# Context projections between the steps of stick attention, an earlier memory attention and a reordered first gated tile

## What is computed

```python
def first_block(...):
    for i in range(2):
        h = rmsnorm(x, mix_norm[i])
        y_mem = memory_cross_attention(q_mem, mem_k, mem_v)
        if i == 0:
            y_main = b_gate * causal_short_conv(c_gate * u, conv_w[i])
        else:
            y_main = stick_breaking_attention(q_sb, k_sh, v_sh)
        x = x + concatenate([y_main, y_mem]) @ w_o[i]
        x = x + swiglu(rmsnorm(x, ffn_norm[i]), w_gate[i], w_up[i], w_down[i])
    return rmsnorm(x, final_norm)

def stick_breaking_attention(q, k, v):          # 12 heads of 64, 128 queries at a time
    z = q @ k.T * scale
    log_not = where(causal, log_sigmoid(-z), 0.0)
    tail = cumsum(log_not, reverse=True) - log_not
    a = where(causal, exp(log_sigmoid(z) + tail), 0.0)
    return a @ v
```

## Time and profile before

| what | value |
|---|---|
| runs | 1219.28, 1216.86, 1215.56 us; median 1216.86 us |
| the profiled execution | 1218.38 us |
| its span | 1217.1 us |
| mean granted clock of TensorE | 0.979 |
| PE busy | 1162.5 us, 96% |
| DVE busy | 833.4 us, 68% |
| ACT busy | 623.2 us, 51% |
| POOL busy | 149.4 us, 12% |
| PE's share of the chain that ended last | 81% |
| DMA engines, share held by the raw loads' queue | 55.6% |
| read from HBM | 219.42 MB, 181 GB/s over the span |

### The profile page before, as it was taken

The page is one execution under the profiler, slowest core; times in us unless marked ns, Lnnn a source line. Parts: engine busy times, 40 slices in busy tenths (PEclk is TensorE's granted clock), DMA queues, the critical chain, the costliest instruction groups (busy, mean ns, idle before and its releaser), DMA issues.

```text
span 1217.1 us, 21837 instructions
## 1 busy us (share of the span) xinstructions
PE 1162.5 (96%) x9014; PEld 1113.4 (91%) x9014; DVE 833.4 (68%) x1278; ACT 623.2 (51%) x938; POOL 149.4 (12%) x111
## 2 busy tenths in 40 slices
PE   8999899999899898999999999999999988999996
PEld 6999899999788788999998898979899988999995
DVE  5677577778774766777778656476645767677775
ACT  5645444445564645444345664655436545555453
POOL 0003000000100012000000000000001032344431
PEclk9999999999998898999999999999999998999998
DMA  8545588777644144777887445354325553555540
GB/s 317 191 158 174 182 268 258 236 251 227 242 132 130 52 163 157 234 247 256 267 270 243 156 156 173 105 160 139 118 88 161 185 177 102 188 177 190 177 153 36
DMA packets 60467, 221.90 MB, mean 182 GB/s; under 512 B 6752, under 2 KB 7008, under 8 KB 59984
## 3 DMA queue, kind: packets, MB, share of 16 engines
q1 hardware_dynamic: 59904, 219.06, 55.6%
q10 hardware_dynamic: 288, 1.05, 0.2%
q0 software_dynamic: 176, 0.39, 0.1%
HBM read 219.42 MB, written 1.05 MB: 181 GB/s over the span
## 4 chain that ended last, share of the span: by engine, by line
PE 81%; DVE 10%; ACT 5%; issue 3%; DMA 1%; SPq 0%; POOL 0%; ACTq 0%; DVEq 0%
PE PS L350 23%; PE PS L352 22%; PE PS L351 22%; PE PS L355 14%; DVE w_lo L1309 3%; ACT w_hi L837 2%; DVE PS L1877 1%; DVE SQ L1575 1%; DMA ARENA<-memT 1%; DVE raw L1331 0%; DVE SQ L1345 0%; DVE ARENA L1345 0%; PE PS L455 0%; DVE H_lo L1355 0%; PE PS L594 0%
## 5 line engine op out<-in xcount | busy, mean ns | idle before, releaser
L1309 DVE TENSOR_TENSOR w_lo<-raw,w_hi 128x1024 fp32r<-128x1024 f32 x325 | 398.9, 1228 | 268.8 <-ACT w_hi L837 268.3
L837 ACT ACTIVATE w_hi<-raw 128x1024 fp32r<-128x1024 f32 x356 | 373.0, 1054 | 144.2 <-PE PS L352 118.4
L350 PE MATMUL PS<-Y_hi,w_hi 128*128 128x256 f32 x1240 | 359.3, 290 | 11.4 <-issue 3.7
L351 PE MATMUL PS<-Y_lo,w_hi 128*128 128x256 f32 x1240 | 354.5, 286 | 0.0
L352 PE MATMUL PS<-Y_hi,w_lo 128*128 128x256 f32 x1240 | 354.3, 286 | 0.0
L350 PEld LDWEIGHTS PS<-Y_hi,w_hi 128*128 128x128 f32 x1240 | 241.7, 195 | 18.0 <-issue 11.8
L351 PEld LDWEIGHTS PS<-Y_lo,w_hi 128*128 128x128 f32 x1240 | 242.1, 195 | 0.4 <-issue 0.2
L352 PEld LDWEIGHTS PS<-Y_hi,w_lo 128*128 128x128 f32 x1240 | 241.7, 195 | 0.0
L350 PE MATMUL PS<-H_hi,w_hi 128*128 128x256 f32 x808 | 232.1, 287 | 7.7 <-DVE G_lo L1436 4.6
L351 PE MATMUL PS<-H_lo,w_hi 128*128 128x256 f32 x808 | 229.1, 284 | 0.0
L352 PE MATMUL PS<-H_hi,w_lo 128*128 128x256 f32 x808 | 229.0, 283 | 0.0
(11 more groups left out here) (207 smaller groups left out, 1323.2 us busy)
## 6 DMA issues: line engine op xcount, KB each, us to landing
raw<-stream SPq DMA_DIRECT2D x404, 512.0 KB, 4.2
ARENA<-memT SPq DMA_DIRECT2D x2, 512.0 KB, 7.6
X<-xT SPq DMA_DIRECT2D x1, 1024.0 KB, 11.2
ARENA<-c_rows SPq DMA_DIRECT2D x2, 512.0 KB, 8.1
ARENA<-memT SPq DMA_DIRECT2D x1, 1024.0 KB, 8.5
ARENA<-ctxT SPq DMA_DIRECT2D x1, 1024.0 KB, 7.3
outT<-ARENA SPq DMA_DIRECT2D x2, 512.0 KB, 2.6
CROW<-c_rows SPq DMA_DIRECT2D x1, 512.0 KB, 10.5
```

The lines of the kernel that those rows point to most:

```text
L350: pe.matmul(o, wh, xh, start=start, stop=False, skip_group_check=True)
L351: pe.matmul(o, wh, xl, start=False, stop=False, skip_group_check=True)
L837: act.activation(w_hi[n % RING][:], raw[at][:], ACT.Copy).then_inc(*mark("hi", n))
L1309: dve.tensor_tensor(w_lo[n % RING][:], raw[raw_of("slot", n)][:], w_hi[n % RING][:], ALU.subtract).then_inc(*mark("lo_dve", n))
```

## The change

It does five things.

- The stages `ctx_lr` and `ctx_k` (5 slots) move from behind `ffn1` to between `kv_v1` and `w_o1`. There they are slots 122 to 126, and steps of stick attention run beside them. Stick outputs become a side task of their own (`stick_outputs`) in PSUM banks 2 and 3. The context set has its own tiles `CX_hi`, `CX_lo`; its sum of squares runs beside `a_c`, its norm in the tail of `ffn0`.
- Memory attention of layer 1 starts with `b_q` at once, where a step of `nothing` and the norm of `kv` stood ahead of it. On ACT and DVE it is run together with that norm by a new helper `both`. The stick schedule follows it, together with the stick outputs.
- In the first tile of each feed-forward, ACT and DVE do the gated product (`hidden`, `g_hi`, `g_lo`) ahead of the two fills. The silu of the modulation's inputs in `ffn0` comes behind it.
- All dot products with two inputs (mods 0 to 15) are in `ffn0` now, one in each of the first 16 tiles; `ffn1` has the other 32.
- `w_o1` takes its contraction tiles in the order 0, 1, 2, 3, 6, 7, 4, 5. The end of block 1 is paced anew beside the 8 slots of `ctx_v` that are left.

```diff
-          ("kv_v1", 2), ("w_o1", KC), ("ffn1", FFN_SLOTS),
-          ("ctx_lr", 1), ("ctx_k", 4), ("ctx_v0", 4), ("ctx_v1", 4),
+          ("kv_v1", 2), ("ctx_lr", 1), ("ctx_k", 4), ("w_o1", KC), ("ffn1", FFN_SLOTS),
+          ("ctx_v0", 4), ("ctx_v1", 4),
...
+def both(first, second):
+    live = [first, second]
+    while live:
+        live = [task for task in live if next(task, "end") != "end"]
+        yield
...
+    if _l == 0:
+        _now = [_j] if _j < CTX_MODS else []
     else:
-        _now = [CTX_MODS + _one + i for i in range(2 if _l and _j in (11, 13, 15, 17) else 1)]
+        _now = [len(MOD_ORDER) + _i for _i in range(2 if _j % 2 and _j > 2 else 1)]
```

The program of PE:

```diff
                     emptied[b] = [("ma_exp", l, 7)]
-                yield from nothing(6)
-                pe.wait_ge(*past("ma_prob", l, 7))
-                claim(*bs)
                 for h in range(MEMH):
+                    if h % 2 == 0:
+                        yield from pace.to(7 + l + h // 2)
+                    if h == 0:
+                        pe.wait_ge(*past("ma_prob", l, 7))
+                        claim(*bs)
...
-            def stick_output():
+            def stick_outputs():
+                pace = Pace()
                 for c in range(MC):
-                    b = 4 + c // 2
+                    b = 2 + c // 2
                     if c % 2 == 0:
+                        yield from pace.to(14 + c)
                         claim(b)
...
             kept = 0
-            side.tasks[:0] = [nothing(1)]
-            side.tasks += [memory_attention(1), stick_schedule(stick_group, lambda: kept)]
+            side = Side(memory_attention(1), both(stick_schedule(stick_group, lambda: kept), stick_outputs()))
             project("b_q", MC, H, lambda i: ("q", i), side, None, 2)
...
             project_tokens("kv_v1", 256, Y, (2, 3), ("vs", 1), side)
+            project("ctx_lr", 1, CX, lambda i: ("lr", 0), side, [norm_low("ctx", k) for k in range(KC)])
+            project("ctx_k", GH, CX, lambda i: ("kb", 0, i), side)
             side.finish()
-            pe.wait_ge(*past("vs", 1))
-            stick_output()
-            side = Side(context_rms())
...
-            project("w_o1", KC, H, lambda i: ("added", 1, i), side, y_ready)
-            side.finish()
-            ffn(1, Side(nothing(KC + 1)))
+            project("w_o1", KC, H, lambda i: ("added", 1, i), None, y_ready, order=(0, 1, 2, 3, 6, 7, 4, 5))
+            ffn(1)
```

The same place on ACT and DVE, where `both` also wraps memory attention, and DVE's feed-forward:

```diff
             kept = 0
-            side.tasks[:0] = [nothing(1)]
-            side.tasks += [memory_attention(1), stick_schedule(stick_group, lambda: kept)]
+            side.tasks = [both(memory_attention(1), chain(*side.tasks)),
+                          both(stick_schedule(stick_group, lambda: kept), stick_outputs())]
...
                     dve.tensor_tensor(GF[:], PS[:, 2 * p, 0:T], RS[:, 0], ALU.mult).then_inc(*mark("gate", l, j))
-                    fill()
+                    if j:
+                        fill()
...
                     hidden_low(l, j)
+                    if j == 0:
+                        fill()
+                        fill()
```

More of the change, by code:

```diff
@@ L1 @@
 from contextlib import ExitStack
+from itertools import chain
 import numpy as np
@@ L52 @@
 for _l, _j in ((_l, _j) for _l in range(2) for _j in range(FC)):
[L53 to L56, removed]
+    if _l == 0:
+        _now = [_j] if _j < CTX_MODS else []
     else:
-        _now = [CTX_MODS + _one + i for i in range(2 if _l and _j in (11, 13, 15, 17) else 1)]
+        _now = [len(MOD_ORDER) + _i for _i in range(2 if _j % 2 and _j > 2 else 1)]
     MOD_ORDER += _now
     MODS_AFTER[AT[f"ffn{_l}"] + (RING + 1 + 2 * _j if _j < 2 else RING + 3 * _j)] = _now
-assert sorted(MOD_ORDER) == list(range(NMOD))
-CTX_FFN1 = next(a for a in MODS_AFTER[AT["ffn1"] + RING + 1])
+assert MOD_ORDER == list(range(NMOD))
 LOADS = []
@@ L278, in build @@
         RS_COLS = small[:, 32:34]
-        RS_AT = {"mem0": 1, "mix0": 0, "mix1": 0, "ctx": 1, "final": 0, "norm1": 1, "out": 0}
+        RS_OF = {"mem0": RS[:, 1], "mix0": RS[:, 0], "mix1": RS[:, 0], "ctx": LR[:, 1], "final": RS[:, 0],
+                 "norm1": RS[:, 1], "out": RS[:, 0]}
         def gain(name, c):
@@ L328, in sync_program @@
                     sp.dma_start(MEM, memT).then_inc(*mark("mem_in", by=16))
[L329 to L332, removed]
+                if (kind, n) == ("slot", AT["a_c"] + 4):
                     sp.dma_start(CTX, ctxT).then_inc(*mark("ctx_in", by=16))
@@ L359, in slot, with tall @@
                 return n % RING
-            def tall(o, h, ready=None, within=None):
+            def tall(o, h, ready=None, within=None, order=range(KC)):
                 nonlocal n
                 r = slot()
-                for k in range(KC):
+                for k in order:
                     if ready:
@@ L387, in wide, with project @@
                 n += 1
-            def project(stage, count, h, release, side=None, ready=None, steps=1):
+            def project(stage, count, h, release, side=None, ready=None, steps=1, order=range(KC)):
                 assert n == AT[stage], (stage, n)
@@ L507, in ffn @@
                 for j in range(2, FC):
-                    beside = tail if j >= FC - 4 else None
+                    beside = tail if j >= FC - 6 else None
                     gate_up(l, j, side=beside)
@@ L1214, in act_program @@
             act.dma_start(WS, sgu_wT).then_inc(*mark("late_in", 1, by=16))
-            side = Side(context_rms())
-            project("w_o1", KC, left, side, then=residual_square(1, H2, lambda c: gain("ffn1", c)))
-            side.finish()
+            project("w_o1", KC, left, then=residual_square(1, H2, lambda c: gain("ffn1", c)))
             inverse_rms("res1")
             act.preload_act_table(ACT.Silu)
-            act.wait_ge(*past("c_in", 2))
-            act.activation(CTX_ROW, CTX_ROW, ACT.Silu).then_inc(*mark("c_silu", 2))
-            ffn(1, Side(norm_his("ctx", Y2, lambda c: SH1(c, 1), CSQ)))
+            ffn(1)
             exp_set()
@@ L1397, in memory_attention @@
                 dve.tensor_scalar(nmx, mx, -HD ** -0.5, None, ALU.mult).then_inc(*mark("ma_max", l))
-                yield from nothing(3)
+                yield from pace.to(4)
                 dve.wait_ge(*past("ma_exp", l, 7))
@@ L1546, in block1_end @@
                                              ALU.mult).then_inc(*mark("x_final", c))
-                    if c % 2:
-                        yield
-                yield from nothing(3)
+                    if c == 3:
+                        yield from pace.to(4)
+                yield from pace.to(8)
                 dve.wait_ge(*past("x_final", KC - 1))
```

193 lines of the change are left out of this document (100 added, 93 removed).

## The result

| | before | changed kernel |
|---|---|---|
| runs | 1217.78 us median (1215.56 to 1219.28) | 1293.69 us median (1292.70 to 1294.15) |
| ratio | | 1.0628, 95% interval 1.0613 to 1.0643 |
| profiled execution, span | 1218.38, 1217.1 | 1292.70, 1291.4 |
| mean granted clock | 0.979 | 0.961 |

The forecast was 1289 us with a range of 1265 to 1312: the change makes the kernel 6.3% slower.

The account below looks back on a forecast made before the run. PE bounds the kernel, busy 96% of the span. 54.3 + 30 - 11.3 + 1.9 - 1.8 - 6.1 - 1.4 + 6.9 = +72.5 on 1218.4 profiled gives 1290.9, median 1289 us, range 1265 to 1312.

Parts of the forecast that it names:

- Stick attention beside the slots: Slots 111 to 126: PE waits a whole round trip for stick operations on DVE, twelve stops of 3 us or more, +54.3 us.
- The clock: Behind the stick attention stops: slow matmuls at TensorE's lower clock, twelve stops at 2.5 us each, +30 us, bounds 14 and 52.
- the three rows: Three long waits in the kernel before, whose slow matmuls behind them cost 1.2, 2.6 and 2.7 us.
- The rival in which the lower level holds throughout: Slots 112 to 126: the lower clock level holds all through, 52 us in place of 30, 1311 us; chance 0.13.
- The stick groups' tail: Behind slot 121: waits of 7.3 us and slow matmuls of 4.0 us leave, -11.3 us.
- memory attention: Layer 1: four pieces of kv norm between maximum and probabilities on DVE lengthen the wait of 3.8, +1.9 us.
- ffn0, -3.2, ffn1, -6.1: Shorter waits and less slow clock: ffn0's start -1.8 us and end -1.4, ffn1's start -6.1.
- The end of block 1: Last additions to norm1's last rest: 8 slots cover it instead of 13, waits 5.4 and slow clock 1.5, +6.9 us.
- Context norm and dot products: Moved to other places, with a two-input dot product in each ffn0 tile: no cost, zero.
- The clock between the slots: Sign: granted clock between slots 112 and 126 under 0.75.
- The stops were to lie between 375 and 460 us: Sign: PE's eleven waits of 3.5 to 6 us on DVE lines 1495 and 1506 all fall between these times.
- The others: Signs: lines 1495 and 1506 hold 45 to 55 us, L1518 one of 3, ffn1's first-tile wait gone, PE near 92%.

Follow-up runs that it names:

- e2: Changed kernel with both() not yielding after its last task, and PE's stick schedule one step later (distance of two slots): 1212.47 us, ratio 0.9953 to before.
- e1: Changed kernel with both() not yielding after its last task, so ACT and DVE start the stick schedule one step earlier: 1224.78 us, ratio 1.0056 to before.
- e9: e6 and e7 together, on top of e2: 1202.30 us, ratio 0.9880 to before.
- e6: e2 with memory attention's transposes, output and end of layer 1 one step later on all engines: 1207.99 us, ratio 0.9930 to before.
- e8: Changed kernel with only PE's stick schedule one step later, both() as it is: 1227.75 us in a single run.
- e3: Changed kernel with useless matmuls on PE ahead of its waits at z(1) to z(5) and tails(0) to tails(5): 1272.84 us in a single run.
- e7: e2 with ctx_k's four slots back behind ffn1 and block 1's end paced as in the kernel before: 1206.04 us, ratio 0.9909 to before.

## Why the prediction was right, and where it was off

The mechanism and its size came out as written; the median was 4.7 us above the forecast of 1289, the profiled execution 1.8 above its 1290.9.

1. *Stick attention beside the slots, +54.3.* Measured 57.1 by the timeline, in the eleven stops of 3.85 to 6.15 us named, one of 2.93 and one of 0.56. The term took PE to start when the operation on DVE ends. PE starts 0.36 us after z_kept (386.71 to 387.07) and 0.14 after log_not (tails(0): from 397.58 to 397.72), 2.6 in eleven stops. The same stands in the kernel before: z_kept from 415.71, 0.95 long, and z(4) at 417.02; log_not's last operation ends at 419.19, and tails follow at 419.33. I hadn't put it into the sum.
2. *The clock, +30.* Measured 24.7. That is 2.2 for each of eleven stops, since the twelfth costs none, where I took 2.5 for twelve; the mean of the three rows, 2.2, which I raised for the stops' closeness, was the better guess. The work behind a stop does leave the slow stretch in time: in the fence above the matmuls are 0.12 us apart again at 392.17, 5 us behind the stop's end. The rival in which the lower level holds throughout would have been 52 (49 with its own 0.21 and 0.12), and falls. The three slow rows have a clock of 0.50 to 0.55, where I wrote 0.56. The Trainium skill ("TensorE: Matmul & The Clock Gate", on HAM oscillation) has each tile behind a long wait start at half clock; the trace agrees for eleven of the twelve stops. The price worked out from its example, an estimate of 0.84 per stop, is under half of what this case shows.
3. *The stick groups' tail, -11.3,* and *memory attention, +1.9.* The wait went from 3.78 to 5.58, +1.8. The whole stretch is +70.6, so 70.6 - 57.1 - 24.7 - 1.8 = -13.0 is left for the rest. 1.0 of it is not the tail's: the same work behind memory attention's wait, slow at first, takes 11.5 us, and 12.5 in the kernel before and in e2. That leaves -12.0 for the tail. e2 has the stretch behind slot 121 without a wait.
4. *ffn0, -3.2, ffn1, -6.1.* Measured -3.1 and -6.5. ffn1's first tile shows one wait of 0.36:

```profile
560.65 0.35 PE L358 MATMUL PS<-Y_hi,w_hi 128*128 128x256 f32 x1 [0.36 <-DVE w_lo L1317]
```

5. *The end of block 1, +6.9.* Measured +11.0, within its bounds of 0 to 12. The waits in it are

```profile
743.25 2.33 PE L363 MATMUL PS<-SQ,consts 128*32 128x256 f32 x16 [1.02 <-ACT SQ L849]
...
746.17 0.70 PE L363 MATMUL PS<-RS,consts 128*128 128x256 f32 x2 [0.59 <-ACT RS L859]
...
753.69 1.33 PE L363 MATMUL PS<-SQ,consts 128*32 128x256 f32 x8 [1.22 <-ACT SQ L849]
...
776.44 0.39 PE L358 MATMUL PS<-Y_hi,w_hi 128*128 128x256 f32 x1 [2.64 <-DVE Y_lo L1356]
```

with three of 0.17, 6.0 in all, against 0.95 before: +5.0, where I had taken 5.4. The clock was the mis-sized part. I had taken 1.5 for it, and it is 4.0, all behind the last wait, the one of 2.64: from lr's first matmul to the queries it takes 25.4 us, 18.6 before, and 2.8 of the difference is waits. The granted clock is 1.00 from 743.2 to 773 in spite of the waits there, and 0.51 from 777.66 to 784.00. Of the last 2.0, 1.3 are sums over the partitions whose matmuls come in pieces.

6. *Context norm and dot products, 0.* ffn0 and ffn1 show no cost. But the context's sums, which I had let drop, cost 2.4: up to ffn0 PE is 3.8 us later (0.7 of it from the first loads, before any changed instruction), and w_o1 gets back only 1.4, since a wait of 0.81 for the last addition now ends it.

Errors of opposite sign (-5.3 for the clock, -0.7 for the tail and -1.0 behind memory attention's wait; +2.8, +4.1 and +2.4) nearly cancel. That the sum is better than its terms is luck.

Two things were off beside the sizes. The cause was half told: I named the helper's last yield alone. It is worth 69 us and leaves a distance of one (e1, 1224.8); the kernel before had two, and only with PE's schedule a step later too is the loss gone (e2, 1212.5). And two of the signs did not come as written. The clock between the slots was to be under 0.75 and is 0.77 to 0.79. The stops were to lie between 375 and 460 us and run on to 523; my own terms, 65 us of work, 54 of waits and 30 of clock, already made the stretch 150 long. The others came: 45.9 us stand under the lines 1495 and 1506, in nine waits, and two more of their kind, 7.7 us, under ACT's line; L1518 has one of 2.9, and PE's share is 92%.

**Faster than both kernels.** e9 at 1202.3 us is 1.2% under the kernel before. It has the reordered tile, the earlier memory attention with one step more for its probabilities, `ctx_lr` alone moved, block 1's end paced as before, the mended helper, and stick attention at a distance of two.

## What to carry to other kernels

Where three engines run the same steps by hand, write down for every wait of the bound engine which of its own results the awaited operation needs in the end, the queue ahead of it included; if that is the one just finished, the engine stands for the whole round trip, however idle the others are. A helper that costs one engine one step is invisible in a diff read engine by engine; the orders side by side show it. And price a stop twice: once for the wait, once for the slow matmuls behind it, here 57 and 25 us.

## What the runs showed of the hardware

- From the end of an operation on DVE, as the profile shows it, to the start of the matmul that waits for it lie 0.36 us behind z_kept (in the changed kernel at 387.07, in the kernel before at 417.02) and 0.14 behind log_not (397.72 and 419.33).
- The eleven stops of 3.9 to 6.2 us cost 2.2 us of slow matmuls each on the mean, at 0.21 us per 128x256 instead of 0.12. The ratio is 1.8 and not the 2 of the two clock levels.
- Behind shorter stops the clock falls in one profile and not in another, though the program up to there is the same. One stop at ffn0's start is 2.23 or 2.24 us long in the changed kernel and in seven of its variants. The clock granted in the 2 us behind it was 0.50 in the changed kernel, e1 and e6, 0.59 in e9, 0.89 in e8, and 1.00 in e2, e3 and e7. The work behind it, up to PE's next wait, took 1.3 us less in e2 than in the changed kernel, so that much of a profile's reading at such a place can be chance.
- Matmuls of no use in the stops made the kernel 20 us faster (e3), with the granted clock at 0.97 instead of 0.77 in the same 127 us.
- The wait for memory attention, 5.6 us, shrank by 2.9 when one slot was put in front of it, and the whole kernel by 4.5 (e2 to e6): the slow stretch behind it shrank too, by 1.3.
